# Rotation of queries and keys: row tiles 2 and 3 on GpSimd, tiles 0 and 1 on VectorE

## The chip, the cores and the metric

One core of a Trainium2 chip. The metric is the device time of one execution in microseconds (us). Each engine (TensorE, VectorE, ScalarE, GpSimd, SyncE) works through its own list of instructions in order; they meet at semaphores only.

## The reference, cut to what matters

The program is one block of a first kind and then two layers of a second kind, on a sequence of 512 tokens with 1024 features, in float32. The change lies in each of the two layers, in the branch with grouped queries:

```
def gqa_branch(q, k, v, qn_g, kn_g):
    q = rms_norm(q.reshape(bsz, s, B_HEADS_2, B_DH), qn_g)     # 8 heads of 64
    k = rms_norm(k.reshape(bsz, s, B_KV, B_DH), kn_g)          # 2 heads of 64
    ang_r, ang_c = axial_rope_angles(s)
    q = axial_rope(q, ang_r, ang_c) * (B_DH ** -0.5)           # x1*c - x2*sn, x2*c + x1*sn
    k = axial_rope(k, ang_r, ang_c)
```

Everything of this is per token: a head's 64 numbers are scaled by one factor of the norm, and quarters of 16 are mixed in pairs with a cosine and a sine.

## The kernel before, in words

**Dense blocks.** All products with the weights are blocks (AQ, AG, BQ, BKV, AK, AV, G00, ...; the order is `ORDER2`, line 128). A block of 512 columns has four units of 256 rows of the weight. A unit goes through three stages: SyncE loads it (three buffers); ScalarE copies its rounded part to `wH` (L871), which waits until TensorE has finished the unit two before it, since there are two buffers; VectorE subtracts to get the rest, `wL` (L1328). TensorE then waits on `w_lo` (line 526) and makes 24 matmuls of 512 columns (L539 or L542). The other engines prepare one unit ahead (`LOOK` = 1): while TensorE is at unit i, ScalarE and VectorE split unit i+1, and after each split they do what a function `between(i)` holds. So the side work of one step stands, in the order of VectorE's and ScalarE's lists, ahead of the next split.

**Rotation.** The query projection (block BQ) and the key projection (BKV) are copied by ScalarE into `qraw` and `kraw`, parts of the buffer `gbuf`, tokens on the partitions, four row tiles of 128 tokens. Sums of squares go to `st40`. While TensorE is at block AK, VectorE's `ak_between` takes the root's reciprocal at i = 1 (L1974) and calls `rotate(t)` for t = 0, 1, 2 at i = 1, 2, 3; `rotate(3)` stands in `av_between` at i = 0. One `rotate` is 7 instructions for the queries (128 x 512: a product with the cosine table L1914, four products of 128 x 128 with the sine table L1920, a sum L1924, a product with the norm's factor L1925) and the same 7 for the keys on a quarter of the width. It uses `rope_c` and `rope_s` in `gbuf` as scratch.

**After it.** While TensorE is at block AV, VectorE's `av_between` does four convolutions (`conv(4)` to `conv(7)`, lines 1886 to 1898), each followed by ScalarE's tanh (L1163) and VectorE's `conv_silu` (L1904). TensorE transposes the rotated queries after unit 1 of AV and the keys after unit 2 (`b_transposes`, L573); it waits there for `ropeq_ready` four times. ScalarE copies the transposes out (L1211, L1217) between its tanh and its next split. Then comes the stage `mlstm`, whose first dense group waits for the first unit of G00.

**GpSimd** fills zeros (L477, L478) and issues DMAs of tables; in this part of a layer its list is empty.

Of the kernel before, what the change touches and what calls it, by code (L numbers as in the profile page):

```python
# [23 lines left out]
ALU = mybir.AluOpType  # L24
AX = mybir.AxisListType.X

P = 128
SEQ = 512
# [207 lines left out]
def build(nc, a, out):  # L236
# [8 lines left out]
    with ctx:  # L245
# [73 lines left out]
        def view(t, off, shape):  # L319
# [54 lines left out]

        names = """
            x_tile0 x_tile1 x_tile2 x_tile3 ident_norm consts masks_ready landed0 landed1 landed2 w_hi w_lo groups free0 free1 free2 free3
            act_step dve_step gp_step
            norm_sq norm_ms norm_sd xn_ready tp_done tp_hi tp_free x_ready x_done
            sc_done hi_done split_done mx_done ex_done pt_done ptev pv_done y_done
            tab_dma0 tab_dma1 mb_done e_done qk_done p_done o_done hh_done  # L380
# [89 lines left out]
        @block.gpsimd  # L470
        def _(pool):

            def zeros(after):

                if after:
                    pool.wait_ge(S["groups"], after.groups_end)
                pool.memset(k_low[0][DH:P, :].bitcast(F32), 0.0)  # L477
                pool.memset(k_low[1][0:DH, :].bitcast(F32), 0.0).then_inc(S["low_zero"], 1)  # L478
            zeros(None)
            pool.wait_ge(S["lvl_done"], 4 * LEVELS)  # L480
            pool.dma_start(view(gflat, 0, (4, P)), a["w_sT"]).then_inc(S["gp_step"], 16)
            for i, name in enumerate(("gmlp_ln_g", "gmlp_ln_b")):
                pool.dma_start(gflat[:, 512 + 256 * i:768 + 256 * i], bcast_rows(a[name][0], 256)).then_inc(
                    S["gp_step"], 16)
            pool.dma_start(view(gflat, 1024, (4, P)), a["keep4"]).then_inc(S["gp_step"], 16)

            pool.wait_ge(S["y_ready"], 1)
            pool.dma_start(yflat[:, 0:D], bcast_rows(a["final_norm_g"], D)).then_inc(S["gp_step"], 16)
            for l in range(DEPTH):
                gqa0 = 32 + 96 * l  # L490
                nat0, diff0 = gqa0 + 32, gqa0 + 64

                def zero_halves(after):
                    zeros(by_name[(l + 1, after)])
                zero_halves("U01")
                for h in range(HEADS):
                    if h == 2:
                        zero_halves("U11")

                    pool.wait_ge(S["mx_done"], gqa0 + 1 if h < 2 else nat0 + 4 * (h - 1))  # L500
                    for half in range(2):
                        off = l * (RPB_LEN + 2 * RPB_PAD) + RPB_PAD + RPB_LEN - 1 - RPB_HEAD * h - (14 - half) * 31 - 78
                        src = bass.AP(tensor=a["rpb_rev"].tensor, offset=off, ap=[[1, 64], [31, 14], [1, 64]])
                        pool.dma_start(tab[64 * half:64 * half + 64, h % 2, :].rearrange("p (e k) -> p e k", e=14),
                                       src).then_inc(S[f"tab_dma{h % 2}"], 16)
                for h in range(4):
                    if h == 2:
                        zero_halves("U21")
                    pool.wait_ge(S["mx_done"], nat0 + 28 + 4 * h if h < 2 else diff0 + 12 + 4 * (h - 2))
                    pool.dma_start(tab[:, h % 2, :], a["alibi"][h]).then_inc(S[f"tab_dma{h % 2}"], 16)  # L510

            pool.wait_ge(S["late"], 2)
            pool.dma_start(yflat[:, 0:D], bcast_rows(a["final_g_2"], D)).then_inc(S["gp_step"], 16)
# [3 lines left out]
        def _(pe):  # L517
# [255 lines left out]
            for l in range(DEPTH):  # L773
                L = l + 1

                def B(*names):
                    return [by_name[(L, name)] for name in names]

                xn_transposes()
                dense(L, "AQ", KD)  # L780
                dense(L, "AG")
                dense(L, "BQ")
                dense(L, "BKV")

                pe.wait_ge(S["rows_ready"], l + 1)
                for t in range(NT):
                    for w, row in enumerate((row_w, row_m)):
                        mm = pe.transpose(bank[TP][:, (2 * t + w) * GATE_ROWS:(2 * t + w + 1) * GATE_ROWS],
                                          row[:, t * P:(t + 1) * P], ident[0:GATE_ROWS, 0:GATE_ROWS])
                mm.then_inc(S["rowt_done"], 1)  # L790
                dense(L, "AK")

                def b_transposes(i):

                    if i == 1:
                        pe.wait_ge(S["rowt_read"], l + 1)
                        transposes(qraw, 4, "ropeq_ready", NT)
                    elif i == 2:
                        transposes(kraw, 1, None, 0)
                dense(L, "AV", between=b_transposes)  # L800
                pe.wait_ge(S["tp_free"], n.at("tp"))
                mlstm(l, side_groups(B("G00", "G01"), B("CQ")[0]))
                dense(L, "CQ", start=1)
                dense(L, "AO")
                dense(L, "CK", stop=3)
                transposes(ytok, 4, "y_ready", NT)
                dense(L, "CK", start=3)
                dense(L, "U00", 4)
                dense(L, "U01")
                dense(L, "CV")  # L810
                softmax(gqa_items(), v2b, side_groups(B("G10", "G11"), B("DQ")[0]))
                dense(L, "DQ", start=1, stop=3)
                pe.wait_ge(S["y_done"], n.at("ys"))
                transposes(ytok, 4, None, 0)
                dense(L, "DQ", start=3)
                dense(L, "U10", 4)
                dense(L, "U11")
                dense(L, "DK")
                evacuated(B("CV")[0])
                softmax(nat_items(), v1, side_groups(B("G20", "G21"), B("DV")[0]))  # L820
                dense(L, "DV", start=1, stop=3)
                pe.wait_ge(S["y_done"], n.at("ys"))
                transposes(ytok, 4, None, 0)
                dense(L, "DV", start=3)
                dense(L, "U20", 4)
                dense(L, "U21")
                dense(L, "G30", stop=1)
                evacuated(B("DV")[0])
                softmax(diff_items(), v2, side_groups(B("G30", "G31"), done=1, idle=DIFF_IDLE))
                transposes(ytok, 4, "y_ready", 0, each=1)  # L830
                dense(L, "U30", 4)
                dense(L, "U31")
                transposes(merged, (0, 1, 2, 3), "y_ready", NT)
                transposes(merged, (4, 5, 6, 7), "y_ready", NT)
                dense(L, "O0", KD)
                dense(L, "O1")
                xn_transposes()
                for name in ffn_order():
                    if name.startswith("FD") and name.endswith("0"):
                        banks = B("FU" + name[2])[0].banks  # L840
                        pe.wait_ge(S["hid_ready"], n("hid_ready", banks))
                    dense(L, name, KD if name == "FG0" else 0)
# [457 lines left out]
        def _(dve):  # L1300
# [527 lines left out]
            for l in range(DEPTH):  # L1828
# [128 lines left out]
                def ak_between(i):  # L1957
                    if i == 0:
                        dve.wait_ge(S["sq_ready"], n("sq_ready"))
                        group_sums(st40[:, 32:40], sbufPT[:, 0, :], 8)  # L1960
                        n("sq_taken", NT)
                        V.tensor_scalar(st40, st40, 1.0 / DH, EPS, ALU.mult, ALU.add).then_inc(S["ms_ready"], 1)

                        dve.wait_ge(S["rowt_done"], l + 1)
                        rows_t = bank[TP][:, 0:8 * GATE_ROWS].rearrange("p (t w r) -> p t w r", t=NT, w=2)
                        for w, dst in ((0, wcol), (1, mcol)):
                            for d in range(2):
                                ins = V.tensor_copy(dst.rearrange("p (t d h) -> p t d h", t=NT, d=2)[:, :, d, :],
                                                    rows_t[:, :, w, 32 * d:32 * d + 4])
                        ins.then_inc(S["rowt_read"], 1)  # L1970
                    else:
                        if i == 1:
                            dve.wait_ge(S["sd_ready"], n("sd_ready"))
                            then(V.reciprocal(st40, st40))  # L1974
                        rotate(i - 1)
                dense(L, "AK", between=ak_between)

                def av_between(i):
                    if i == 0:
                        rotate(3)  # L1980
                    if i < 3:
                        conv(4 + i)
                    if i in (1, 2):
# [213 lines left out]
```

## Time and profile before

| | us |
|---|---|
| Time, median of 3 runs (lowest, highest) | 2710.51 (2709.81, 2711.15) |
| The profiled execution, its own time | 2716.0 |
| Its span, first to last instruction | 2714.2 |
| TensorE busy with matmuls | 2621.3 |
| VectorE busy | 1471.4 |
| ScalarE busy | 1133.4 |
| GpSimd busy | 40.3 |
| TensorE's mean granted clock, share of full speed | 0.986 |

A timeline row gives the start, the duration, the engine, the source line, the operation, what it writes and reads, how many instructions the row holds, and, in brackets, the idle time ahead of it and what ended it. Matmuls overlap: the distance of their starts, not their duration, is their price. Two durations that overlap by a tenth of a microsecond on VectorE are the same effect.

### The profile page before, as it was taken

The page shows a single profiled execution, that of the slowest core. Times are in us where ns is not written, and L with a number is a line of the kernel's source. Part 1 is how long each engine was busy: PE and PEld are TensorE (multiplying, and loading weights), DVE is VectorE, ACT ScalarE, POOL GpSimd, SP SyncE. Part 2 cuts the span into 40 slices and gives each one's busy share as a digit, 9 for nine tenths or more (in the row PEclk, how much of TensorE's full clock was granted, in tenths as well). Part 3 has the DMA queues.
Part 4 walks back from the last instruction along what each step waited for, and adds up shares of the span by engine and source line. Part 5 has one row for each costly group of instructions (what it writes and reads, how often), then busy time and mean ns, then how long its engine had stood idle before and what let it go on. Part 6 is the DMA issues. An engine that isn't in the chain of part 4 may idle for free.

```text
span 2714.2 us, 33991 instructions
## 1 busy us (share of the span) xinstructions
PE 2621.3 (97%) x13218; PEld 2194.7 (81%) x13218; DVE 1471.4 (54%) x2719; ACT 1133.4 (42%) x1946; POOL 40.3 (1%) x64
## 2 busy tenths in 40 slices
PE   7998979999999999999999899999999999999997
PEld 6887868788888887878888787888888887788886
DVE  5656558554545558444444576544456485444444
ACT  4426344333644647332222344335446373322222
POOL 0000000000000000000000000000001000000000
PEclk9999989999999999999999999999999999999999
DMA  4320213122223421223332222233134221233322
GB/s 139 86 63 28 72 55 93 55 78 93 61 63 86 78 86 53 91 81 100 94 101 86 79 86 63 63 95 75 55 90 77 88 72 63 86 94 101 93 86 93
DMA packets 118431, 216.98 MB, mean 80 GB/s; under 512 B 14272, under 2 KB 21824, under 8 KB 118272
## 3 DMA queue, kind: packets, MB, share of 16 engines
q1 hardware_dynamic: 114528, 201.97, 24.5%
q0 software_dynamic: 3744, 12.85, 3.0%
q8 instruction: 106, 1.74, 0.3%
q14 instruction: 53, 0.43, 0.0%
HBM read 212.69 MB, written 2.10 MB: 79 GB/s over the span
## 4 chain that ended last, share of the span: by engine, by line
PE 88%; DVE 7%; ACT 3%; issue 2%; DMA 0%; ACTq 0%; DVEq 0%
PE bank L539 41%; PE bank L542 28%; PE bank L633 6%; PE bank L622 3%; PE bank L602 2%; PE bank L573 2%; PE bank L603 2%; PE bank L662 1%; PE bank L679 1%; DVE wL L1328 1%; PE bank L716 1%; ACT wH L871 1%; ACT sbufS L910 1%; DVE gbuf L1920 0%; DVE sbufS L1895 0%
## 5 line engine op out<-in xcount | busy, mean ns | idle before, releaser
L1328 DVE TENSOR_TENSOR wL<-wraw,wH 128x1024 fp32r<-128x1024 f32 (+1 forms) x388 | 460.1, 1186 | 718.7 <-ACT wH L871 717.3
L871 ACT ACTIVATE wH<-wraw 128x1024 fp32r<-128x1024 f32 (+1 forms) x388 | 398.4, 1027 | 928.6 <-PE bank L539 500.5
L539 PE MATMUL bank<-wH,hH 128*128 128x512 f32 (+1 forms) x1248 | 500.7, 401 | 7.2 <-DVE wL L1328 3.8
L539 PE MATMUL bank<-wH,hL 128*128 128x512 f32 (+1 forms) x1248 | 479.4, 384 | 0.0
L539 PE MATMUL bank<-wL,hH 128*128 128x512 f32 (+1 forms) x1248 | 478.8, 384 | 0.0
L542 PE MATMUL bank<-hH,wH 128*128 128x512 f32 x1208 | 473.4, 392 | 3.2 <-ACT set L889 1.6
L542 PE MATMUL bank<-hH,wL 128*128 128x512 f32 x1208 | 470.3, 389 | 0.0
L542 PE MATMUL bank<-hL,wH 128*128 128x512 f32 x1208 | 470.2, 389 | 0.0
L539 PEld LDWEIGHTS bank<-wH,hH 128*128 128x128 f32 x1248 | 236.5, 189 | 60.8 <-issue 7.5
L539 PEld LDWEIGHTS bank<-wH,hL 128*128 128x128 f32 x1248 | 236.5, 190 | 48.5 <-issue 3.3
L539 PEld LDWEIGHTS bank<-wL,hH 128*128 128x128 f32 x1248 | 235.9, 189 | 47.9
L542 PEld LDWEIGHTS bank<-hH,wH 128*128 128x128 f32 x1208 | 226.8, 188 | 51.2 <-issue 3.6
L542 PEld LDWEIGHTS bank<-hH,wL 128*128 128x128 f32 x1208 | 226.7, 188 | 47.6
L542 PEld LDWEIGHTS bank<-hL,wH 128*128 128x128 f32 x1208 | 226.9, 188 | 46.0
L539 PE MATMUL bank<-wH,yH 128*128 128x512 f32 x608 | 238.7, 393 | 5.7 <-DVE yL L2103 4.8
L539 PE MATMUL bank<-wH,yL 128*128 128x512 f32 x608 | 237.4, 391 | 0.0
L539 PE MATMUL bank<-wL,yH 128*128 128x512 f32 x608 | 237.3, 390 | 0.0
L633 PE MATMUL bank<-set,sbufPT 128*128 128x64 f32 (+1 forms) x1440 | 187.3, 272 | 7.5 <-DVE merged L1471 5.2
L633 PEld LDWEIGHTS bank<-set,sbufPT 128*128 128x128 f32 x1440 | 178.2, 193 | 12.1 <-issue 10.4
L539 PEld LDWEIGHTS bank<-wH,yH 128*128 128x128 f32 x608 | 114.8, 189 | 31.5 <-DVE yL L2103 5.6
L539 PEld LDWEIGHTS bank<-wL,yH 128*128 128x128 f32 x608 | 114.7, 189 | 24.1
L539 PEld LDWEIGHTS bank<-wH,yL 128*128 128x128 f32 x608 | 115.0, 189 | 23.6
(295 smaller groups left out, 2837.2 us busy)
## 6 DMA issues: line engine op xcount, KB each, us to landing
wraw<-in_w_in_dram SPq DMA_DIRECT2D x180, 512.0 KB, 3.6
wraw<-in_w_ffn_down_dram SPq DMA_DIRECT2D x44, 512.0 KB, 3.5
wraw<-in_w_ffn_gate_dram SPq DMA_DIRECT2D x40, 512.0 KB, 3.6
wraw<-in_w_ffn_up_dram SPq DMA_DIRECT2D x40, 512.0 KB, 3.6
wraw<-in_w_out_dram SPq DMA_DIRECT2D x24, 512.0 KB, 3.5
tab<-in_rpb_rev_dram POOLq DMA_DIRECT2D x32, 224.0 KB, 6.3
wraw<-in_w_up_a_dram SPq DMA_DIRECT2D x8, 512.0 KB, 3.4
wraw<-in_w_up_b_dram SPq DMA_DIRECT2D x8, 512.0 KB, 3.5
```

Source lines behind the costliest of these rows:

```text
L539: mm = pe.matmul(bank[t][:, 0:b.cols], act_part[:, k, t * P:(t + 1) * P], w_part[:, kk, :], start=first, stop=last)
L542: mm = pe.matmul(bank[b.bank0 + t][:, :], w_part[:, kk, t * P:(t + 1) * P], act_part[:, k, :], start=first, stop=last)
L573: mm = pe.transpose(bank[SC + i % TR_BANKS][:, t * P:(t + 1) * P], src[:, t, k * P:(k + 1) * P], ident[:, :])
L602: pe.matmul(dst[:, 0:kmax], q_split[slot][:, tok], k_twice[slot][:, 0:kmax], start=True, stop=False)
L603: mm = pe.matmul(dst[:, 0:kmax], q_split[slot][:, tok], k_low[slot][:, 0:kmax], start=False, stop=kind != "fox")
L622: mm = pe.transpose(bank[TP][:, c * P:(c + 1) * P], sbufS[:, y % 3, c * P:(c + 1) * P], ident[:, :])
L633: mm = pe.matmul(bank[PV][:, 0:w], sbufPT[:, y % 2, c * P:(c + 1) * P], v[:, c, c0:c0 + w], start=c == 0, stop=c == nk - 1)
L662: pe.matmul(bank[SC + i % 2][:, lo:hi], k1[:, h, j * P:(j + 1) * P], q1[:, h, lo:hi], start=True, stop=True).then_inc(S["qk_done"], 1)
L679: mm = pe.matmul(dst[:, 0:P + 1], pmat[:, (c - 1) % 2, sj, j * P:(j + 1) * P], v1a[:, sj, h, :], start=sj == srcs[0], stop=sj == srcs[-1])
L716: mm = pe.matmul(bank[SC + h][:, tok], kl[r, h // 2, tok], ql[r, h // 2, tok], start=True, stop=True)
L871: A(wH[:, u % W_SLOTS, 0:width], wraw[:, u % RAW_SLOTS, 0:width], ACT.Copy).then_inc(S["w_hi"], 1)
L1328: V.tensor_tensor(wL[:, u % W_SLOTS, 0:width], wraw[:, u % RAW_SLOTS, 0:width], wH[:, u % W_SLOTS, 0:width].bitcast(F32), ALU.subtract).th ...
```

## The change

GpSimd gets the rotation of tiles 2 and 3, in both layers, with scratch in `ytok` (`yflat`), which nothing else uses at that point. It starts when the rows of `ytok` are read (`rowt_read`) and the norm's factors are there (`norm_inv`, which VectorE now raises behind the reciprocal). Every instruction of GpSimd but the last of a tile waits for the one ahead of it through a semaphore. VectorE keeps tiles 0 and 1; its step i = 3 of AK and the beginning of its step i = 0 of AV are without a rotation. TensorE waits for two tiles of each engine ahead of the transposes.

```diff
@@ GpSimd, in the loop over the layers, ahead of zero_halves("U01")
+                pool.wait_ge(S["rowt_read"], l + 1)
+                pool.wait_ge(S["norm_inv"], l + 1)
+                pool_c, pool_s = yflat[:, 0:SEQ], yflat[:, SEQ:2 * SEQ]
+                for t in (2, 3):
+                    for z, heads, tc, ts, r in ((qraw[:, t, :], 8, cq_t, sq_t, st40[:, 8 * t:8 * t + 8]),
+                                                (kraw[:, t, :], 2, ck_t, sk_t, st40[:, 32 + 2 * t:34 + 2 * t])):
+                        w = heads * DH
+                        xc, xs, z3 = (v.rearrange("p (h d) -> p h d", h=heads)
+                                      for v in (pool_c[:, 0:w], pool_s[:, 0:w], z))
+
+                        def then(ins):
+                            ins.then_inc(S["pool_rope"], 1)
+                            pool.wait_ge(S["pool_rope"], ropes("pool_rope"))
+                        then(pool.tensor_tensor(xc, z3, tc[:, t, :].unsqueeze(1).to_broadcast([P, heads, DH]), ALU.mult))
+                        for lo in (0, 16, 32, 48):
+                            sw = lo ^ 16
+                            then(pool.tensor_tensor(xs[:, :, lo:lo + 16], z3[:, :, sw:sw + 16],
+                                                    ts[:, t, lo:lo + 16].unsqueeze(1).to_broadcast([P, heads, 16]),
+                                                    ALU.mult))
+                        then(pool.tensor_tensor(xc, xc, xs, ALU.add))
+                        ins = pool.tensor_tensor(z3, xc, r.unsqueeze(2).to_broadcast([P, heads, DH]), ALU.mult)
+                        if heads == 8:
+                            then(ins)
+                    ins.then_inc(S["ropep_ready"], 1)
+                    pool.wait_ge(S["ropep_ready"], 2 * l + t - 1)
@@ TensorE, b_transposes
                         pe.wait_ge(S["rowt_read"], l + 1)
-                        transposes(qraw, 4, "ropeq_ready", NT)
+                        pe.wait_ge(S["ropep_ready"], 2 * (l + 1))
+                        transposes(qraw, 4, "ropeq_ready", 2)
@@ VectorE, ak_between and av_between
                             dve.wait_ge(S["sd_ready"], n("sd_ready"))
-                            then(V.reciprocal(st40, st40))
-                        rotate(i - 1)
+                            V.reciprocal(st40, st40).then_inc(S["norm_inv"], 1)
+                            dve.wait_ge(S["norm_inv"], l + 1)
+                        if i < 3:
+                            rotate(i - 1)
                 dense(L, "AK", between=ak_between)

                 def av_between(i):
-                    if i == 0:
-                        rotate(3)
                     if i < 3:
                         conv(4 + i)
```

## Rows read from the trace of the kernel before

**Rows 1.** The page: busy time by engine; shares of the chain that ended last.
```profile
PE 2621.3 (97%) x13218; PEld 2194.7 (81%) x13218; DVE 1471.4 (54%) x2719; ACT 1133.4 (42%) x1946; POOL 40.3 (1%) x64
...
PE 88%; DVE 7%; ACT 3%; issue 2%; DMA 0%; ACTq 0%; DVEq 0%
```

**Rows 2.** Waits, 425 to 510 us: total us, times, longest.
```profile
PEld bank L539 <- DVE wL L1328: 2.5, 2, 1.7
...
PE bank L539 <- DVE wL L1328: 1.5, 2, 0.9
```

**Rows 3.** Timeline of TensorE, blocks AK and AV of the first layer.
```profile
446.65 0.39 PE L542 MATMUL bank<-hH,wH 128*128 128x512 f32 x1
...
452.09 0.39 PE L539 MATMUL bank<-wH,hH 128*128 128x512 f32 x1
...
457.53 0.39 PE L539 MATMUL bank<-wH,hH 128*128 128x512 f32 x1
...
462.97 1.91 PE L573 MATMUL bank<-ident,gbuf 128*128 128x128 f32 x16
464.63 0.48 PE L539 MATMUL bank<-wH,hH 128*128 128x512 f32 x1
...
470.19 0.60 PE L573 MATMUL bank<-ident,gbuf 128*128 128x128 f32 x4
471.36 0.50 PE L539 MATMUL bank<-wH,hH 128*128 128x512 f32 x1 [0.58 <-DVE wL L1328]
...
479.22 0.50 PE L539 MATMUL bank<-wH,hH 128*128 128x512 f32 x1 [0.90 <-DVE wL L1328]
```

**Rows 4.** Timeline of VectorE, the same stretch.
```profile
438.69 0.69 DVE L1914 TENSOR_TENSOR gbuf<-gbuf,tab 128x512 f32<-128x512 f32 x1
439.30 0.89 DVE L1920 TENSOR_TENSOR gbuf<-gbuf,tab 128x128 f32<-128x128 f32 x4
...
441.68 0.29 DVE L1914 TENSOR_TENSOR gbuf<-gbuf,tab 128x128 f32<-128x128 f32 x1
441.89 0.49 DVE L1920 TENSOR_TENSOR gbuf<-gbuf,tab 128x32 f32<-128x32 f32 x4
...
443.06 1.23 DVE L1328 TENSOR_TENSOR wL<-wraw,wH 128x1024 fp32r<-128x1024 f32 x1
...
448.57 1.23 DVE L1328 TENSOR_TENSOR wL<-wraw,wH 128x1024 fp32r<-128x1024 f32 x1
...
454.08 1.23 DVE L1328 TENSOR_TENSOR wL<-wraw,wH 128x1024 fp32r<-128x1024 f32 x1
...
459.58 0.49 DVE L1894 TENSOR_SCALAR sbufS<-set,small 128x512 f32<-128x512 f32 x1
...
463.29 1.23 DVE L1328 TENSOR_TENSOR wL<-wraw,wH 128x1024 fp32r<-128x1024 f32 x1 [1.65 <-ACT wH L871]
...
470.08 1.23 DVE L1328 TENSOR_TENSOR wL<-wraw,wH 128x1024 fp32r<-128x1024 f32 x1 [2.99 <-ACT wH L871]
...
477.94 1.22 DVE L1328 TENSOR_TENSOR wL<-wraw,wH 128x1024 fp32r<-128x1024 f32 x1 [1.29 <-ACT wH L871]
```

**Rows 5.** Timeline of ScalarE, the same stretch.
```profile
452.78 1.05 ACT L871 ACTIVATE wH<-wraw 128x1024 fp32r<-128x1024 f32 x1
461.68 0.63 ACT L1163 ACTIVATE sbufPT<-sbufS 128x512 f32<-128x512 f32 x1 [7.84 <-DVE sbufS L1897]
462.21 1.04 ACT L871 ACTIVATE wH<-wraw 128x1024 fp32r<-128x1024 f32 x1
```

**Rows 6.** Timeline of GpSimd, the start of the program.
```profile
0.28 0.11 POOL L2188 MEMSET const-float32-1.0<- 128x1 f32 x1
...
0.75 0.52 POOL L477 MEMSET yH<- 64x512 f32 x1 [0.29 <-POOLq L2188]
```

**Rows 7.** Timeline of VectorE, the second layer.
```profile
1631.96 0.49 DVE L1894 TENSOR_SCALAR sbufS<-set,small 128x512 f32<-128x512 f32 x1
```

More of the change, by code:

```diff
@@ L376, in build @@
             x_tile0 x_tile1 x_tile2 x_tile3 ident_norm consts masks_ready landed0 landed1 landed2 w_hi w_lo groups free0 free1 free2 free3
-            act_step dve_step gp_step
+            act_step dve_step gp_step norm_inv pool_rope ropep_ready
             norm_sq norm_ms norm_sd xn_ready tp_done tp_hi tp_free x_ready x_done
@@ L485, in _ @@
             pool.dma_start(view(gflat, 1024, (4, P)), a["keep4"]).then_inc(S["gp_step"], 16)
+            ropes = Count()
             pool.wait_ge(S["y_ready"], 1)
```

## The prediction

> **What bounds the kernel now.** I read the page first: TensorE is busy for 97% of the span and carries 88% of the chain that ended last, VectorE 7% of it [rows 1]. A change that takes work off VectorE can therefore give back only the little time in which TensorE stands still for VectorE. The waits of the stretch in which the change lies come next: between 425 and 510 us TensorE waits for VectorE's `wL` twice, 1.5 us in sum, and its weight loads, the same two stops seen from the other side, 2.5 us [rows 2]. The reader is to see how small the prize is: about 2 us in each of two layers.
>
> The timelines say where those stops come from. In block AK a unit takes TensorE 5.44 us (446.65 to 452.09, and to 457.53) [rows 3]. VectorE's `wL` for the units that start at 446.65, 452.09 and 457.53 end at 444.29, 449.80 and 455.31 [rows 4]: 2.4, 2.3 and 2.2 us early. So the three rotations in block AK cost nothing now; the matmuls hide them, with 2.2 us to spare. `rotate(3)` is different. It ends at 459.58, and only then does the first convolution start [rows 4]; ScalarE has stood idle for 7.84 us when its tanh starts at 461.68, and its next split of a weight stands behind that tanh, at 462.21 [rows 5]. VectorE's `wL` then ends at 464.52, just as TensorE comes out of the transposes at 464.63. The next two are late: 471.31 against transposes of the keys that are over at about 470.7, and 479.16 against a group that is due behind the matmuls that precede it [rows 3, 4]. The delay that `rotate(3)` sets up is handed on from split to split, and these are the two stops. The second layer runs the same pattern 1172.38 us later (1631.96 against 459.58) [rows 4, 7].
>
> **The change part by part.**
>
> VectorE loses `rotate(2)` and `rotate(3)`. One rotation costs it 4.37 us (438.69 to 443.06) [rows 4]. The first of the two is worth nothing, being hidden. The second lets the first convolution start at 455.3 in place of 459.58, and everything that is handed on from it (tanh, split, `wL`) moves forward: ScalarE's split could start at about 458.2, four microseconds ahead of 462.21 [rows 5]. The two late `wL` then come at least 1.5 us earlier, since each is now held by TensorE's transposes and ScalarE's copies in place of the convolution; the stops of 0.58 and 0.90 us go [rows 3]. Gain: between 1.5 and 2.5 us per layer by the two rows of the waits [rows 2]; I take 2.0, so 4.0 us in two layers. Behind that TensorE is late for nothing here, being its own limit.
>
> GpSimd gains 28 dependent instructions per layer: per tile 3 of 512 elements, 4 of 128, 3 of 128 (keys) and 4 of 32. The trace of before never shows GpSimd reading from SBUF, so each price is bounded. A memset of 512 takes 0.52 us and one of a single element 0.11 [rows 6]: 0.11 fixed and 0.41 per pass over 512. Two inputs and an output are at most three such passes one after another, 1.34 us, and two if output and input overlap, 0.93; VectorE does it in 0.69 [rows 4]. I take 2.5 passes, 1.14 us; by the same rule 0.37 for 128 elements and 0.17 for 32. A tile is then 3 x 1.14 + 4 x 0.37 + 3 x 0.37 + 4 x 0.17 = 6.7 us. The step through the semaphore is between nothing and the 0.29 us that GpSimd idled ahead of its first memset [rows 6]; I take 0.1, 1.4 us per tile. Two tiles are 16.2 us, bounds 8.7 (VectorE's own price) and 2 x (7.7 + 4.1) = 23.6. They start at 438.7, behind the reciprocal, and are due at 462.97, when the transposes start [rows 3]: left alone, GpSimd ends at about 455, and even the upper bound, 462.3, is just in time. The page GPSIMD Engine Reference of the Trainium skill (section Performance versus the Vector engine) gives 4497 ns for an add of 2048 float32, an estimate of 1.12 us for 512; the sum would be the same by it.
>
> The new waits: `norm_inv` takes the place of an equal wait. TensorE's wait for `ropep_ready` stands ahead of the transposes; behind it are units 2 and 3 of AV and the whole stage `mlstm`, so if GpSimd is late, TensorE pays one for one. GpSimd's next work, zeros and table DMAs, comes some 190 us later, and SyncE's queue is not touched: nothing.
>
> **What decides** is whether GpSimd and VectorE can read SBUF side by side. VectorE's rotations, its `wL` and two of three instructions of a convolution have two inputs from SBUF, as GpSimd's all have. The trace cannot show it. From below, they don't disturb each other: 0. From above, they take turns, each instruction holding the other's up for its whole length. Then `rotate(0)` beside GpSimd's first tile takes 4.4 + 6.7 = 11.1 us and ends at 449.8, and with one more GpSimd instruction (0.6) and 1.23 its `wL` ends at 451.6, where 446.65 was wanted: TensorE stands for 5.0 us. `rotate(1)` beside the second tile ends at about 461.6, the `wL` behind it at 462.8, where 457.1 is wanted: 5.7 more. From there VectorE is ahead and the 2.0 of gain is had: 8.7 us lost per layer. If only the part of each instruction without its fixed 0.1 us holds the other up, 28 times 0.1 = 2.8 us fewer per pair of tiles, the pair takes 8.3, the two stops are 2.0 and 3.3, and the loss is 3.3 us. I forecast turns, at the middle, 6.0 us per layer and 12 us in all. The page SBUF — State Buffer of the Trainium skill (section Practical consequences) says that a VectorE instruction with two SBUF inputs contends with a GpSimd instruction that reads SBUF, whole instruction against whole instruction. No run here shows it yet; by that rule the taking of turns happens, and its loss tends to the upper end.
>
> The sum: the profiled execution took 2716.0 us, 5.5 above the median of 2710.5; with the change 2728.0 profiled, and 2722.5 in the runs.
>
> **The rivals.**
>
> *No contention.* GpSimd is done at 455, the prize of 4.0 us is had: 2706.5. For it: all of VectorE's durations here are regular, and each engine has its list; nothing in the trace speaks against it. At 2 x 2.5 it is 5.0 us, which still is no more than 0.2% of the time (5.4 us, about what a measurement of this kernel can tell from no change), so this case is mostly "within" and touches "faster" only if the earlier convolutions give more than the two stops show.
>
> *VectorE goes first and GpSimd starves.* If GpSimd gets SBUF only when VectorE leaves it, it begins at 449.8, behind the two rotations and their `wL`. Until the transposes VectorE holds SBUF for two more `wL` and two convolutions, 6.7 us; 16.2 + 6.7 puts the end at 472.7, 9.7 us behind 462.97, less 2.0: 7.7 us per layer, 2726. The stop then stands at the transposes (L573), not at `wL`. Against it: VectorE has short gaps between its instructions, into which GpSimd can step.
>
> *GpSimd is slow by itself.* At its upper bounds of 23.6 us it uses all its cover; a first use that costs some microseconds more would put 0 to 5 us on the transposes of the first layer and cancel the gain: 2708 to 2712. Its mark would be a stop at L573 with VectorE's durations unchanged.
>
> *The work doesn't move.* Not possible: `rotate` is called for i < 3 alone.
>
> **How the numbers follow.** Turns 0.50 (2717 to 2728, to 2735 with GpSimd at its upper price), starving 0.12, slow GpSimd 0.08, no contention 0.30. The rows alone would give turns and no contention even chances; the page's rule moves it to the first. Slower: 0.50 + 0.12 + a little of the third, 0.63. Within 0.2%: most of no contention and of the third, 0.27. Faster 0.10. The range has to hold both the gain and the turns, 2705 to 2732; the likeliest case's own is 2716 to 2730.
>
> **What would show it.** Right: rows of L1914, L1924, L1925 and L1328 between 438 and 463 that last longer than 0.69 and 1.23 us or start late, TensorE idle ahead of units 3 of AK and 0 of AV for `wL` (2 to 6 us each), no stop at L573, and the two stops at 471 and 479 gone. A mean of a GpSimd product of 512 under 0.9 or over 1.4 us would make the price wrong. VectorE's rows unchanged beside a busy GpSimd would make the whole forecast wrong, and a stop at L573 would name one of the other two.

## The result, and the profile after

| | before | after |
|---|---|---|
| Time, median us (18 runs each) | 2712.14 (2709.78 to 2716.20) | 2719.70 (2714.33 to 2723.84) |
| Profiled execution, its own time, us | 2716.0 | 2715.3 |
| Its span, us | 2714.2 | 2713.6 |

The change makes the kernel slower: ratio 1.0029, 95% interval 1.0022 to 1.0037, that is 7.6 us between the medians. The two profiled executions show no such difference, and the first thing to see is why they can't be held against each other as wholes. The one of before was among its slowest executions, the one of after among its fastest, and they differ by 5.04 us already at the reciprocal ahead of the first rotation (438.26 against 433.22), where the programs are still the same. The granted clock differs there: between 180 and 200 and between 200 and 220 us it is 0.81 and 0.85 in the trace of before, 0.87 and 0.96 in that of after, and TensorE starts 192 matmuls in those 40 us against 213; 21 matmuls at 0.23 us are about 4.8 of the 5.04 us. So I measure each layer from its own landmark: from VectorE's reciprocal to GpSimd's first memset behind block U01. The timelines of VectorE and of GpSimd, kernel before, then after (columns as in [rows 4]):

```profile
438.26 0.40 DVE L1974 RECIPROCAL small<-small 128x40 f32<-128x40 f32 x1
...
655.52 0.52 POOL L477 MEMSET yH<- 64x512 f32 x1 [366.81 <-PE bank L539]
```

```profile
433.22 0.40 DVE L2003 RECIPROCAL small<-small 128x40 f32<-128x40 f32 x1
...
652.46 0.52 POOL L477 MEMSET yH<- 64x512 f32 x1 [194.79 <-PE bank L567]
```

217.26 us before, 219.24 after: 1.98 more. The second layer gives 217.29 and 219.25. This distance, called the layer's stretch below, is the same in both layers to a few hundredths of a microsecond, before and after, where the whole time scatters by six. Between executions it is steady only where the granted clock is; the next run shows that.

Now the stretch itself, in the changed kernel. Its lines lie further down than in the kernel before: `wL` is L1357, the cosine product L1943, the sine products L1949, the sum L1953, the factor L1954; TensorE's two dense lines are L567 and L570. First TensorE's timeline, the rows that answer to [rows 3]:

```profile
441.38 0.39 PE L570 MATMUL bank<-hH,wL 128*128 128x512 f32 x1
443.14 0.50 PE L570 MATMUL bank<-hH,wH 128*128 128x512 f32 x1 [1.37 <-DVE wL L1357]
...
448.49 0.39 PE L570 MATMUL bank<-hH,wL 128*128 128x512 f32 x1
450.85 0.50 PE L567 MATMUL bank<-wH,hH 128*128 128x512 f32 x1 [1.97 <-DVE wL L1357]
...
461.87 1.91 PE L601 MATMUL bank<-ident,gbuf 128*128 128x128 f32 x16
```

Two stops where there were none, ahead of the last unit of AK and the first of AV, both for `wL`. Matmuls start 0.23 us apart, so their price is 443.14 - 441.61 = 1.5 us and 450.85 - 448.72 = 2.1 us. Behind each stop the next matmul starts 0.34 us later and not 0.23, and a unit takes 0.14 us more; with that the two stops cost 3.94 us. So much later do the transposes start, 28.65 us behind the reciprocal where it was 24.71. The stretch as a whole is only 1.98 us longer: the other 1.96 are had back behind the transposes, where the two stops of before, 0.58 and 0.90 us, are gone. The transposes (L601) start without a wait. Then VectorE, the rows that answer to [rows 4]:

```profile
433.65 0.69 DVE L1943 TENSOR_TENSOR gbuf<-gbuf,tab 128x512 f32<-128x512 f32 x1
434.26 2.25 DVE L1949 TENSOR_TENSOR gbuf<-gbuf,tab 128x128 f32<-128x128 f32 x4
436.55 0.84 DVE L1953 TENSOR_TENSOR gbuf<-gbuf 128x512 f32<-128x512 f32 x1
...
438.64 1.58 DVE L1949 TENSOR_TENSOR gbuf<-gbuf,tab 128x32 f32<-128x32 f32 x4
440.26 1.03 DVE L1953 TENSOR_TENSOR gbuf<-gbuf 128x128 f32<-128x128 f32 x1
441.32 0.50 DVE L1954 TENSOR_TENSOR gbuf<-gbuf,small 128x128 f32<-128x128 f32 x1
441.86 1.23 DVE L1357 TENSOR_TENSOR wL<-wraw,wH 128x1024 fp32r<-128x1024 f32 x1
443.01 0.74 DVE L1943 TENSOR_TENSOR gbuf<-gbuf,tab 128x512 f32<-128x512 f32 x1
...
449.36 3.66 DVE L1357 TENSOR_TENSOR wL<-wraw,wH 128x1024 fp32r<-128x1024 f32 x2
```

The same four products of 128 x 128 take 2.25 us instead of 0.89, the four of the keys 1.58 instead of 0.49. `rotate(0)` takes 8.2 us (433.65 to 441.82) where [rows 4] have 4.37, and `rotate(1)` 6.3 (443.01 to 449.32). The wait does not show as idle time: VectorE counts as busy, its instructions just last longer. The page's busy times therefore say nothing of it: VectorE's 1471.1 us are the 1471.4 of before, though four rotations of 4.4 us have left it. And GpSimd, from its timeline:

```profile
433.77 1.72 POOL L508 TENSOR_TENSOR ytok<-gbuf,tab 128x512 f32<-128x512 f32 x1 [150.27 <-DVE small L2003]
435.57 3.00 POOL L511 TENSOR_TENSOR ytok<-gbuf,tab 128x128 f32<-128x128 f32 x4
...
457.26 0.40 POOL L515 TENSOR_TENSOR gbuf<-ytok,small 128x128 f32<-128x128 f32 x1
```

It works from 433.77 to 457.66, 23.9 us, and is done 4.2 us ahead of the transposes.

### The profile page after: what moved, and what is told of

Read it like the earlier page. It is cut to its first block, busy times and chain, and to the rows that moved or that the text cites. A ratio compares the mean times of both kernels' runs of the same rounds, so it can differ in the third digit from the quotient of the medians.

```text
span 2713.6 us, 33997 instructions
## 1 busy us (share of the span) xinstructions
PE 2616.5 (96%) x13218; PEld 2190.6 (81%) x13218; DVE 1471.1 (54%) x2663; ACT 1134.4 (42%) x1946; POOL 84.0 (3%) x120
## 4 chain that ended last, share of the span: by engine, by line
PE 73%; issue 19%; DVE 5%; ACT 2%; DMA 0%; POOL 0%; ACTq 0%; DVEq 0%; POOLq 0%
PE bank L567 35%; PE bank L570 20%; PE bank L661 5%; PE bank L650 3%; PE bank L630 2%; PE bank L601 2%; PE bank L631 2%; PE bank L690 1%; PE bank L707 1%; PE bank L744 1%; DVE wL L1357 1%; ACT sbufS L939 1%; DVE gbuf L1949 0%; PE bank L682 0%; ACT wH L900 0%
## 5 line engine op out<-in xcount | busy, mean ns | idle before, releaser
L1357 DVE TENSOR_TENSOR wL<-wraw,wH 128x1024 fp32r<-128x1024 f32 (+1 forms) x388 | 462.5, 1192 | 722.7 <-ACT wH L900 721.2
L567 PE MATMUL bank<-wH,hH 128*128 128x512 f32 (+1 forms) x1248 | 500.9, 401 | 8.2 <-DVE wL L1357 4.8
L570 PE MATMUL bank<-hH,wH 128*128 128x512 f32 x1208 | 473.7, 392 | 5.6 <-DVE wL L1357 3.1
L567 PE MATMUL bank<-wH,hL 128*128 128x512 f32 (+1 forms) x1248 | 478.9, 384 | 0.0
L567 PE MATMUL bank<-wL,hH 128*128 128x512 f32 (+1 forms) x1248 | 478.6, 383 | 0.0
L570 PE MATMUL bank<-hH,wL 128*128 128x512 f32 x1208 | 470.4, 389 | 0.0
L570 PE MATMUL bank<-hL,wH 128*128 128x512 f32 x1208 | 470.2, 389 | 0.0
L567 PEld LDWEIGHTS bank<-wH,hH 128*128 128x128 f32 x1248 | 236.1, 189 | 60.9 <-issue 8.0
L567 PEld LDWEIGHTS bank<-wH,hL 128*128 128x128 f32 x1248 | 236.2, 189 | 48.9 <-issue 3.8
L567 PEld LDWEIGHTS bank<-wL,hH 128*128 128x128 f32 x1248 | 235.6, 189 | 47.8
L570 PEld LDWEIGHTS bank<-hH,wH 128*128 128x128 f32 x1208 | 226.8, 188 | 54.4 <-DVE wL L1357 4.8
L570 PEld LDWEIGHTS bank<-hH,wL 128*128 128x128 f32 x1208 | 226.7, 188 | 47.4
L570 PEld LDWEIGHTS bank<-hL,wH 128*128 128x128 f32 x1208 | 226.9, 188 | 46.1
L567 PE MATMUL bank<-wH,yH 128*128 128x512 f32 x608 | 238.0, 391 | 5.7 <-DVE yL L2132 4.8
L567 PE MATMUL bank<-wH,yL 128*128 128x512 f32 x608 | 237.3, 390 | 0.0
L567 PE MATMUL bank<-wL,yH 128*128 128x512 f32 x608 | 237.0, 390 | 0.0
L567 PEld LDWEIGHTS bank<-wH,yH 128*128 128x128 f32 x608 | 114.6, 189 | 31.4 <-DVE yL L2132 5.6
L567 PEld LDWEIGHTS bank<-wL,yH 128*128 128x128 f32 x608 | 114.6, 188 | 23.9
L567 PEld LDWEIGHTS bank<-wH,yL 128*128 128x128 f32 x608 | 114.6, 188 | 23.7
```

Of the source, the lines that this page charges most:

```text
L567: mm = pe.matmul(bank[t][:, 0:b.cols], act_part[:, k, t * P:(t + 1) * P], w_part[:, kk, :], start=first, stop=last)
L570: mm = pe.matmul(bank[b.bank0 + t][:, :], w_part[:, kk, t * P:(t + 1) * P], act_part[:, k, :], start=first, stop=last)
L1357: V.tensor_tensor(wL[:, u % W_SLOTS, 0:width], wraw[:, u % RAW_SLOTS, 0:width], wH[:, u % W_SLOTS, 0:width].bitcast(F32), ALU.subtract).th ...
```

## The experiments

Each was timed against runs of the kernel before on the same chip. The ratios are those of the comparison; "stretch" is the distance defined above, 217.26 us in the kernel before.

### The changed kernel once more

No edit.

> The changed kernel once more, for a second trace. By its first trace each layer costs 1.98 us more between the reciprocal and GpSimd's zeros behind block U01 (219.24 against 217.26 us), 4 us in all, while the median of the runs is 7.6 us higher. Theory A: the contention of the two engines is the whole cause and the rest is chance in which runs were drawn; the ratio then comes down to about 1.0015 (+4 us). Theory B: the stops of TensorE in block AK also make its granted clock fall in more stretches in some executions, each for a microsecond or two; then the ratio stays near 1.003, and a trace of an execution of 2719 us or more shows granted clock under 1.00 in stretches in which the first trace had 1.00, while the per-layer distance stays 219.2 us.

Ratio 1.0025 (1.0014 to 1.0037), median 2719.43 us over 7 runs. The profiled execution took 2719.9 us, where the first one took 2715.3. Its stops for `wL` are the same to a tenth of a microsecond (1.4 and 2.0 us), but its stretch is 220.83 us in the first layer and 220.85 in the second: 1.6 us more than in the first trace. The stretches by tens of microseconds (columns: us, then busy us and instructions of TensorE, its weight loads, VectorE, ScalarE and GpSimd, then the granted clock, DMA share, GB/s) show why, first trace and then second:

```profile
440.00:450.00 10.00, 7.50 (x32) 5.55 (x30) 9.69 (x21) 3.94 (x6) 8.93 (x14) 1.00 0.18 52
450.00:460.00 10.00, 9.15 (x40) 7.60 (x41) 7.98 (x8) 2.15 (x3) 7.04 (x9) 1.00 0.37 107
```

```profile
440.00:450.00 10.00, 6.79 (x29) 4.99 (x27) 9.72 (x18) 4.39 (x6) 8.98 (x14) 1.00 0.18 52
450.00:460.00 10.00, 9.85 (x36) 8.01 (x37) 6.43 (x7) 1.69 (x2) 6.33 (x9) 0.83 0.37 107
```

In the second trace the granted clock is 0.83 between 450 and 460 us, a part of them at 1.2 GHz instead of 2.4: from 451.20 to 454.18 us, right behind the second stop, its matmuls start 0.43 us apart instead of 0.23. TensorE starts 36 matmuls where it started 40. The second layer has the same. So the clock of theory B is what was seen, in one trace of two: 4.0 us from the stops, and 3.2 us from the clock behind them. Its other half was wrong, for the stretch does not stay at 219.2 us. The ratio alone doesn't decide, since its interval just reaches theory A's 1.0015.

The traces of all runs speak for the stops as what the fall follows. Four have both stops of 1.4 us and 2.0, or 0.8 and 2.65: the two of the change, and the runs with products beside and with the early start below. Three of these four have the fall, in both layers. The other seven, that of the kernel before among them, have fewer or shorter stops between 430 and 480 us (the longest pair is 0.99 and 1.55 us, beside the memsets below), and none has the fall there.

### The rotations taken off VectorE, and done nowhere

Tiles 2 and 3 are left out of the computation.

```diff
-                        rotate(i - 1)
+                        if i < 3:
+                            rotate(i - 1)
...
-                    if i == 0:
-                        rotate(3)
...
-                        transposes(qraw, 4, "ropeq_ready", NT)
+                        transposes(qraw, 4, "ropeq_ready", 2)
```

> The kernel before with the rotation of tiles 2 and 3 left out on VectorE and done nowhere; TensorE waits for two tiles. This is the change without GpSimd: what taking the work off VectorE is worth by itself. Forecast theory: the two stops of TensorE of 0.58 and 0.90 us per layer go, 2.0 us per layer, the time falls by 4.0 us (between 3 and 5). Rival (VectorE's work there was hidden altogether): within 1 us.

Ratio 0.9986 (0.9977 to 0.9995), 2708.99 against 2711.79 us. The stretch is 215.24 us, 2.02 less than before, and TensorE waits for `wL` nowhere between 425 and 510 us. The prize is what the prediction took, 2.0 us per layer; the interval of the ratio, 1.4 to 6.2 us in all, holds the 4.0 but could not give it so closely.

### GpSimd's products beside the whole kernel before

VectorE rotates all four tiles and TensorE waits for those four; GpSimd makes its 28 instructions on `x` and writes to scratch, and VectorE waits for it only ahead of `mlstm`.

```diff
-                    for z, heads, tc, ts, r in ((qraw[:, t, :], 8, cq_t, sq_t, st40[:, 8 * t:8 * t + 8]),
-                                                (kraw[:, t, :], 2, ck_t, sk_t, st40[:, 32 + 2 * t:34 + 2 * t])):
+                    for z, heads, tc, ts, r in ((x[:, t, 0:SEQ], 8, cq_t, sq_t, st40[:, 8 * t:8 * t + 8]),
+                                                (x[:, t, SEQ:SEQ + P], 2, ck_t, sk_t, st40[:, 32 + 2 * t:34 + 2 * t])):
...
-                        ins = pool.tensor_tensor(z3, xc, r.unsqueeze(2).to_broadcast([P, heads, DH]), ALU.mult)
+                        ins = pool.tensor_tensor(xs, xc, r.unsqueeze(2).to_broadcast([P, heads, DH]), ALU.mult)
```

> The kernel before whole (VectorE rotates all four tiles), and beside it GpSimd makes the same 28 instructions per layer from the same moment, on other data (x) and with its result in scratch, so that TensorE never waits for it. Turns on SBUF: VectorE's rotations beside it stretch from 4.4 to 6 to 8 us as in the changed kernel, the wL behind them is late in every unit of AK and the first of AV, and with no rotation taken off the time rises by more than with the change: 6 to 12 us per layer, 12 to 24 in all. No contention (the cost of the change is only TensorE's wait on GpSimd): no change within 2 us.

Ratio 1.0056 (1.0043 to 1.0069), 2727.58 against 2711.79 us: 15.8 us, with nothing waiting for GpSimd before the `mlstm` stage, and with GpSimd reading other data (`x` in place of `gbuf`). The forecast was 12 to 24. Its VectorE timeline begins as in the change:

```profile
437.55 2.26 DVE L1948 TENSOR_TENSOR gbuf<-gbuf,tab 128x128 f32<-128x128 f32 x4
...
441.95 1.59 DVE L1948 TENSOR_TENSOR gbuf<-gbuf,tab 128x32 f32<-128x32 f32 x4
```

So the contention is shown by itself, apart from every new wait of the change. TensorE stops for `wL` five times, for 1.39, 1.97, 0.78, 1.73 and 0.61 us. The stretch is 226.06 us, 8.8 more (17.7 in both layers; the traced execution took 2729.3 us, 1.7 more than the median), of which the granted clock, 0.83 between 450 and 460 us here too, is a part.

### Writing instead of reading

As in the run ahead, with GpSimd's products replaced by memsets of 128 x 1024 into the same scratch.

```diff
-                    for z, heads, tc, ts, r in (...):
-                        ...
+                    for m in range(22):
+                        ins = pool.memset(yflat[:, 0:D], 0.0)
```

> The kernel before whole, and beside it, from the same moment as in the change, GpSimd makes 22 memsets of 128 x 1024 per layer into scratch, one behind the other by semaphore: as long as its rotations lasted (some 24 us), but writing only. If it is GpSimd's reading of SBUF that holds VectorE up (as the VectorE operations with two SBUF inputs suggest), VectorE's rotations keep 4.37 us and the time stays within 1 us of before. If any GpSimd work on SBUF holds VectorE up, the rotations stretch as in the run with products beside (8.2 and 6.3 us) and the time rises by 10 us or more.

The loop stands inside the one over t, so there were 44 memsets per layer and not 22; they last 45 us, to 482.26, and VectorE waits 3.0 us for them at the start of `mlstm`. That makes the time (ratio 1.0008, 0.9999 to 1.0017; stretch 218.91) useless for the question. The rotations answer it, in VectorE's timeline:

```profile
437.59 0.89 DVE L1934 TENSOR_TENSOR gbuf<-gbuf,tab 128x128 f32<-128x128 f32 x4
438.51 0.69 DVE L1938 TENSOR_TENSOR gbuf<-gbuf 128x512 f32<-128x512 f32 x1
...
462.97 0.86 DVE L1908 TENSOR_SCALAR sbufS<-set,small 128x512 f32<-128x512 f32 x1
463.87 0.75 DVE L1909 SCALAR_TENSOR_TENSOR sbufS<-set,small,sbufS 128x511 f32<-128x511 f32 x1
```

With GpSimd writing all the time, every product of the rotation and every `wL` has its old duration. So GpSimd's writes to SBUF, the on-chip memory in which all these tiles lie, don't hold up VectorE's operations with two inputs there. What its products have and a memset has not is their reading; that one input would do as well as two is not shown, since no run has GpSimd read one. The exception is the convolution's `TENSOR_SCALAR`, one input and one output, which takes 0.74 to 0.93 us where [rows 4] have 0.49.

### GpSimd without VectorE's rotations

Tiles 0 and 1 are left out of the computation.

```diff
-                        if i < 3:
-                            rotate(i - 1)
...
-                        transposes(qraw, 4, "ropeq_ready", 2)
+                        transposes(qraw, 4, "ropeq_ready", 0)
```

> The change with VectorE's two remaining rotations left out (tiles 0 and 1 are rotated nowhere), so that GpSimd's two tiles meet only the splits and the convolutions. This gives GpSimd's own price. My estimate was 1.14 us for a product of 512, 0.1 per semaphore step and 16.2 us for both tiles, where the change shows 23.9 from first start to last end. If most of that excess is waiting for VectorE, the two tiles take 16 to 19 us here and TensorE has no stop for wL in block AK: 2 us per layer less than before. If GpSimd is simply slower than estimated, they take 22 us or more.

Ratio 0.9982 (0.9973 to 0.9991), 2706.88 against 2711.50 us; stretch 215.29, no stop for `wL`. GpSimd works from 434.31 to 455.60, 21.3 us, between my two cases. In block AK VectorE and GpSimd meet only at the splits here, and that shows the mechanism in the open; VectorE, then GpSimd:

```profile
438.13 2.09 DVE L1357 TENSOR_TENSOR wL<-wraw,wH 128x1024 fp32r<-128x1024 f32 x1 [3.97 <-ACT wH L900]
443.50 1.23 DVE L1357 TENSOR_TENSOR wL<-wraw,wH 128x1024 fp32r<-128x1024 f32 x1 [3.28 <-ACT wH L900]
```

```profile
437.85 1.29 POOL L514 TENSOR_TENSOR ytok<-ytok 128x512 f32<-128x512 f32 x1
439.21 1.91 POOL L515 TENSOR_TENSOR gbuf<-ytok,small 128x512 f32<-128x512 f32 x1
...
441.73 1.25 POOL L511 TENSOR_TENSOR ytok<-gbuf,tab 128x32 f32<-128x32 f32 x4
443.06 0.46 POOL L514 TENSOR_TENSOR ytok<-ytok 128x128 f32<-128x128 f32 x1
443.60 1.38 POOL L515 TENSOR_TENSOR gbuf<-ytok,small 128x128 f32<-128x128 f32 x1
...
455.20 0.40 POOL L515 TENSOR_TENSOR gbuf<-ytok,small 128x128 f32<-128x128 f32 x1
```

The `wL` of 438.13 starts while GpSimd's sum runs to 439.14 and takes 0.86 us longer than its 1.23. GpSimd's next product starts at 439.21, while that `wL` runs, and takes 1.91 us, where the change has it at 1.09 when nothing is in its way. At 443.50 VectorE is first: its `wL` keeps 1.23 us, and GpSimd's product of 443.60 takes 1.38 instead of 0.40: it ends at 444.98, as if begun at 444.58, when that `wL` was all but over (444.73). One works, the other waits for it to finish. This is what the page SBUF — State Buffer of the Trainium skill (section Practical consequences) says of two SBUF inputs against a GpSimd instruction that reads; the rows agree.

With the two hold-ups of 0.82 and 0.98 us taken off, GpSimd's first tile is 445.06 - 434.31 - 1.8 = 8.95 us by itself, 17.9 for two. The other 3.4 of the 21.3 us are waits for a split or a convolution.

### Tile 3 alone on GpSimd

```diff
-                for t in (2, 3):
+                for t in (3,):
...
-                        if i < 3:
-                            rotate(i - 1)
+                        rotate(i - 1)
```

with the counts of the semaphores to match.

> The change with tile 3 alone on GpSimd; VectorE rotates tiles 0, 1 and 2. GpSimd's work and so its collisions halve: it runs beside rotate(0) and a part of rotate(1) only. Contention theory: rotate(0) still takes about 8.2 us and the first stop of 1.4 us stays; rotate(1) ends late by that, and the second stop, 2.0 us now, shrinks to under 1; the gain of 2.0 us per layer stays whole, since the rotation in block AV is gone. Per layer 1.4 to 2.4 lost and 2.0 won: within 1 us of before per layer, so 2710 to 2714, and 4 to 7 us faster than the change. If what mattered was which tile is late for the transposes, no difference from the change.

Ratio 0.9993 (0.9984 to 1.0002), 2709.74 against 2711.50 us: not told apart from before, faster than the change. The stretch is 217.53 us. `rotate(0)` is stretched as in the change and the stop of 1.4 us stands; the second is 0.2. That is as forecast, within 0.3 us per layer of before. The gap to the change's median, 10 us, is wider than the 4 to 7 forecast: in two layers the stretches give 3.4 us against the change's first trace and 6.6 against its second, and the rest stays open.

### GpSimd's start ahead of the reciprocal

```diff
-                pool.wait_ge(S["norm_inv"], l + 1)
...
+                        if t == 2 and heads == 8:
+                            pool.wait_ge(S["norm_inv"], l + 1)
                         ins = pool.tensor_tensor(z3, xc, r.unsqueeze(2)...
```

> The change, with GpSimd starting at rowt_read instead of at the norm's reciprocal: only its product with the norm's factor waits for that. It starts about 4 us earlier, in a stretch in which VectorE idles for 3.4 us ahead of a split, so a sixth of its reading meets no VectorE work. Contention theory: the collisions with VectorE fall by about 3 us of GpSimd time, the first stop of 1.4 us shrinks or goes, the second stays between 1 and 2: 1 to 1.5 us less per layer than the change, about 2716. If VectorE is slowed by the number of products that meet and not by when they start, the change's 2719 stays.

Ratio 1.0021 (1.0011 to 1.0030), 2716.08 us. The forecast of about 2716 came out, but the trace does not give it for the reason stated: the stops are 0.80 and 2.65 us in place of 1.4 and 2.0, the same sum, where the second was to stay under 2. GpSimd's head start, 5.0 us and not 4, moved its second tile so that `rotate(1)` met more of it (7.2 us, 442.36 to 449.59). The stretch, 220.97 us, is within 0.14 of that in the second trace of the change, with the same granted clock of 0.83 behind the stops; this traced execution took 2720.7 us, 4.6 more than the median. Whether the 3 us less than the change in the median are real is open, the intervals overlap.

### Two orders of work

If the loss lies in a stretched rotation that stands ahead of a split, spreading it should save it. VectorE's two tiles over its three steps:

```diff
-                        if i < 3:
-                            rotate(i - 1)
+                        if i == 1:
+                            rotate(0, q_only)
+                        elif i == 2:
+                            rotate(0, k_only)
+                            rotate(1, k_only)
+                        else:
+                            rotate(1, q_only)
```

`rotate` is given the part to do, and TensorE waits for four parts in place of two tiles.

> The change, with VectorE's two tiles spread over its three steps of block AK: queries of tile 0, then the keys of both tiles, then queries of tile 1, in place of tile 0, tile 1 and an empty step. GpSimd's work and the number of VectorE's products beside it are the same. If TensorE's stops come from a stretched rotation of 8.2 us that stands ahead of a split with 2.4 us to spare, a step of some 4.6 to 6 us fits, both stops go or fall under 0.5 us, and the gain of leaving rotation in block AV out (2.0 us per layer) stands alone: 2708 to 2710, 10 us less than the change. If the contention costs by its amount wherever it lies, the time stays within 2 us of the change, 2717 to 2721.

Ratio 0.9987 (0.9978 to 0.9996), 2709.12 against 2712.02 us: 10 us less than the change with the same products on the same engines. The stretch is 216.60 us, 2.6 and 4.2 less than in the two traces of the change, so 5.3 to 8.5 of the 10 us lie in the two stretches. Its VectorE timeline, one part and the splits on either side:

```profile
436.69 0.84 DVE L1954 TENSOR_TENSOR gbuf<-gbuf,small 128x512 f32<-128x512 f32 x1
437.56 1.37 DVE L1357 TENSOR_TENSOR wL<-wraw,wH 128x1024 fp32r<-128x1024 f32 x1
438.86 1.38 DVE L1943 TENSOR_TENSOR gbuf<-gbuf,tab 128x128 f32<-128x128 f32 x1
...
443.93 1.38 DVE L1357 TENSOR_TENSOR wL<-wraw,wH 128x1024 fp32r<-128x1024 f32 x1
```

The products are held up as before (1.38 us for one that takes 0.29), yet TensorE has no stop ahead of the last unit of AK or the first of AV. Two small ones remain: 0.47 us ahead of the second unit of AV and 0.28 ahead of the first group of `mlstm`. Against the kernel before, the stretch is 0.66 us shorter and not 2.0: the median fell into the forecast range, but the gain did not stand alone as forecast, and more than half of the 2.9 us between the medians lies outside the two stretches.

And the prize can be had without GpSimd, by one swap in VectorE's list of the kernel before:

```diff
-                    if i == 0:
-                        rotate(3)
                     if i < 3:
                         conv(4 + i)
+                    if i == 0:
+                        rotate(3)
```

> The kernel before, without GpSimd, with one swap in VectorE's list: in the first step of block AV the first convolution comes ahead of the rotation of tile 3. The rotation then ends at about 461.7 us in the trace's time, still ahead of the transposes at 462.97; ScalarE's tanh and its next split start some 4 us earlier. If the prize is the order of work at that place and not VectorE's load, this gets most of what leaving the rotations out gets: 2 to 4 us less than before in all. If the load counts, no change.

Ratio 0.9984 (0.9975 to 0.9993), 2708.33 against 2711.79 us; stretch 215.53, 1.73 less than before, where leaving the rotations out gave 2.02. This is faster than both kernels, with nothing moved to another engine.

## Why the prediction was right, and where its sizes were off

**The prize** was read right: 2.0 us per layer forecast, 2.02 measured with the rotations left out, and 1.73 of it comes from the place of `rotate(3)` in VectorE's list, as the swap shows.

**GpSimd's price** was low: 1.14 us for a product of 512, measured 1.29 (1.09 with the factor); 0.37 for 128 elements, measured 0.46 to 0.52 (0.40 with the factor); 0.17 for 32, measured 0.25 (four with three steps between them are the 1.25 us of 441.73). The step through the semaphore was 0.1, measured 0.08. Two tiles cost 17.9 us in place of 16.2, within the bounds, and the cover of 24 us held even with the contention: no stop at the transposes. I had named a mean over 1.4 us for a product of 512 as the mark of a wrong price; in the change the three kinds have means of 1.50 to 1.73, but these hold the waits for VectorE, as the run without VectorE's rotations shows. *Slow GpSimd* and *starving* fall with that (GpSimd starts at 433.77, beside `rotate(0)`); the stop stands at `wL`, as forecast.

**The taking of turns** was right as a mechanism and wrong in size; this is the term that was mis-sized. I let every VectorE product of a rotation wait for one of GpSimd's, 11.1 us for `rotate(0)` by whole durations and 8.3 without the fixed parts, and took the middle. It took 8.2, and `rotate(1)` 6.3, since VectorE often gets two or more short products done for one of GpSimd's: while it made the 14 of `rotate(0)`, GpSimd got through 8. The `wL` of 441.86 waited for nothing. The stops were 1.5 and 2.1 us, where I had 2.0 to 5.0 and 3.3 to 5.7, so both lie under my lower bounds. With their after-effect they cost 3.94 us where I had 8.0, and less the prize of 2.0 the direct loss is 1.98 us per layer and not 6.0. (My end of `rotate(1)` in the upper case was also added up half a microsecond short: 451.6 and the 4.4 and 6.1 us still to run are 462.1, not 461.6.)

**What the prediction did not name** is the clock. A stop is not over when `wL` arrives: in one of the two traces of the change TensorE's granted clock falls behind the two stops, and that costs 1.6 us more per layer. With 4.0 us direct and up to 3.2 from the clock, 4.0 to 7.2 of the 7.6 us between the medians are accounted for; the rest, 0.4 to 3.6 us, is open. How many executions have the fall can't be read from their times, and why some don't is open. So the forecast of 12 us against 7.6 is nearer than its parts deserve, and that much is luck: the net loss of the stops was three times too large, and the clock was missing.

**No contention**, which had 0.30, is ruled out by the run with products beside. The opening's sentence that the engines meet at semaphores only is therefore too narrow: VectorE and GpSimd also meet at SBUF.

## What to carry to other kernels

Before moving elementwise work from VectorE to GpSimd, look at what else VectorE does in that stretch: where both have two inputs in SBUF they waited for each other here instruction by instruction, and this shows in longer durations, not in idle time. The price was paid only where a stretched piece stood ahead of something that TensorE was due to need; the same products, spread over three steps, cost 10 us less in the median. And ask first whether the order of VectorE's own list holds the prize: here one swap got it.

## What the runs showed of the hardware that was not expected

The wait of one engine for the other is visible to a tenth of a microsecond on both, as an instruction lengthened by the rest of the other's (2.09 us in place of 1.23, 1.38 in place of 0.40). GpSimd's memsets leave VectorE's products alone but stretch a `TENSOR_SCALAR` of 128 x 512 from 0.49 to as much as 0.93 us. And two stops of TensorE of 1.4 and 2.0 us, or 0.8 and 2.65, were followed, in three of four traces, by a granted clock of 0.83 between 450 and 460 us, which in the change cost 1.6 us per layer, nearly as much again as the net loss of 1.98 itself.
